# Another order of the last passes of three feed-forward norms: four low parts ahead of a reciprocal, two high parts ahead of a square root

## The chip, the cores and the metric

The kernel runs on one core of a Trainium2 chip. The metric is device time in microseconds (us), the median of several executions. The engines are TensorE (PE in the profile; its weight loads are PEld), VectorE (DVE), ScalarE (ACT), GpSimd (POOL) and SyncE (SP), which issues the loads of the weights.

## The reference

A sequence of 512 tokens with 1024 features goes through a first block of two layers and then a second block of one layer. Only the first block's feed-forward parts and the norms behind them matter here; all is float32.

```python
def layer_norm(x, g, b):
    mu = jnp.mean(xf, axis=-1, keepdims=True)
    var = jnp.mean(jnp.square(xf - mu), axis=-1, keepdims=True)
    return ((xf - mu) * lax.rsqrt(var + LN_EPS)).astype(x.dtype) * g + b
...
for l in range(DEPTH):        # DEPTH = 2
    x = layer_norm(DEEPNORM_ALPHA * x + 0.5 * swiglu_ffn(x, ffn1...), ln1_g[l], ln1_b[l])
    x = layer_norm(DEEPNORM_ALPHA * x + hybrid_mixer(x, ...), ln2_g[l], ln2_b[l])
    x = layer_norm(DEEPNORM_ALPHA * x + 0.5 * swiglu_ffn(x, ffn2...), ln3_g[l], ln3_b[l])
```

## The kernel before

The activations stay in SBUF with the features on the partitions: `x` is eight tiles (k = 0 to 7, `KT` = 8) of 128 features by the tokens. A float32 product is made of three products of shorter numbers: each weight and each activation is split into a high part (`w_hi`, `x_hi`) and a low part (`w_lo`, `x_lo`), and TensorE adds high by high, low weight by high, and high weight by low.

**The norm.** `LayerNorm` works in two parts of 256 tokens, so that the second part's statistics can be taken while the first part is already being used. The diff, and this text, number the sixteen pieces 0 to 7 (part 0, tile k) and 8 to 15 (part 1). For a part, ScalarE squares the mean (`act_mean2`), VectorE makes the variance (`dve_variance`, L843), ScalarE takes the root (`act_root`, L802) and VectorE the reciprocal (`dve_inverse`, L850). Then each piece passes four steps: `centre` on VectorE (L855, subtracts the mean), `scale` on VectorE (L862, times gain and reciprocal), `act_out` on ScalarE (L809, adds the bias and writes the high part `x_hi`), and `lower` on VectorE (L869, writes the low part `x_lo`). Every engine executes its instructions in the order in which they are written, and waits on semaphores for the others. `centre` waits for the reciprocal of its part, `scale` for its own piece's `centre`, also where both run on VectorE. After the pieces ScalarE adds the bias to `x` itself (`act_moved`, L817).

**Who reads the pieces.** The next stage begins with a group of five output tiles (`pe_group`, L458 and L470). TensorE takes the pieces in the order 0 to 15: for each, the five tiles' high weights by `x_hi` of the piece, then by `x_lo` of it. For the pairs 0, 1 and 8, 9 it does three of the tiles for both pieces first and then the other two. It waits for high(piece) before the first and for low(piece) before the second. Then it multiplies the low weights by `x_hi` (L470), with no further need of the norm.

**Which norms.** `finish_act` and `finish_dve` of `LayerNorm` write the order for the norms of class `FfnNorm`. There are three: behind the first feed-forward of layer 0 (in front of a mixer), behind the second of layer 0 (in front of a feed-forward) and behind the first of layer 1 (in front of a mixer). The mixers' norms and the norm between the two blocks have orders of their own, which the diff does not touch. In the stretch of the diff the other work on VectorE's queue is `dve_split` (L350, low part of a weight tile, which frees the raw tile for SyncE's next load) and `dve_z_last` (L876); on ScalarE's it is `act_split` (L339, high part of a weight tile).

Of the kernel before, what the change touches and what calls it, by code (L numbers as in the profile page):

```python
# [24 lines left out]
KT = D // P  # L25
# [216 lines left out]
def build(nc, t):  # L242

    ctx = ExitStack()
    with ctx:
# [84 lines left out]
        def act_split(until):  # L330

            while turn["act"] <= min(until, len(plan) - 1):
                u = turn["act"]
                turn["act"] += 1
                n, r, s = plan[u][3] * P, u % RAW_SLOTS, slot[u]
                act.wait_ge(*loaded[r].at(u))
                if slot_before[u] is not None:
                    act.wait_ge(*used(slot_before[u]))
                nc.scalar.copy(w_hi[s][:, 0:n], w_raw[r][:, 0:n]).then_inc(*w_high.inc(u))  # L339

        def dve_split(until):

            while turn["dve"] <= min(until, len(plan) - 1):
                u = turn["dve"]
                turn["dve"] += 1
                if u in on_pool:
                    continue
                n, r, s = plan[u][3] * P, u % RAW_SLOTS, slot[u]
                dve.wait_ge(*w_high.at(u))
                nc.vector.tensor_tensor(  # L350
                    w_lo[s][:, 0:n], w_raw[r][:, 0:n], w_hi[s][:, 0:n].bitcast(F32),
                    ALU.subtract).then_inc(*w_low_dve.inc(u))
# [416 lines left out]
        class LayerNorm(Norm):  # L769
# [50 lines left out]
            def finish_act(self):  # L820
                self.act_ready()
                self.act_square_last(0)
                self.act_mean2(0)
                self.act_root(0)
                act_split(self.u_next + 1)
                self.act_out(0, 0)
                self.act_out(1, 0)
                act_split(self.u_next + GROUP)
                self.act_square_last(1)
                act_split(self.u_next + GROUP + 1)  # L830
                self.act_mean2(1)
                self.act_out(2, 0)
                self.act_root(1)
                for k in range(3, KT):
                    self.act_out(k, 0)
                for k in range(KT):
                    self.act_out(k, 1)
                self.act_moved()
# [58 lines left out]
            def finish_dve(self):  # L897
                centre, scale, lower = self.passes()
                self.dve_z_last(0)
                self.dve_variance(0)  # L900
                self.dve_inverse(0)
                centre(0, 1)
                scale(0)
                centre(2)
                scale(1, 2)
                centre(3, 4, 5, 6)
                lower(0, 1)
                self.dve_z_last(1)
                centre(7)
                scale(3, 4, 5)  # L910
                lower(2)
                self.dve_variance(1)
                scale(6, 7)
                self.dve_inverse(1)
                lower(3, 4)
                centre(8, 9)
                lower(5, 6)
                scale(8)
                centre(10, 11)
                scale(9)  # L920
                centre(12)
                scale(10)
                lower(7, 8)
                scale(11, 12)
                lower(9, 10)
                dve_split(self.u_next + 1)
                centre(13, 14)
                lower(11)
                scale(13, 14)
                centre(15)  # L930
                scale(15)
                lower(12, 13, 14, 15)
# [2657 lines left out]
```

## Time and profile before

| what | us |
|---|---|
| median of 3 runs | 3092.43 |
| lowest and highest | 3090.99, 3094.99 |
| the profiled execution's own time | 3093.18 |
| span of its trace, first to last instruction | 3091.9 |
| TensorE busy in the span | 3044.0 |
| VectorE busy | 1422.7 |
| ScalarE busy | 1158.2 |

The profiled execution took 0.75 us more than the median, and 1.28 us of it lie around the span. A busy TensorE is not TensorE at its peak, since matmuls are pipelined; a gap in its weight loads is the plainer sign of a wait. Times on the timelines are us from the start of the span. In a timeline row the first number is the start, the second the time to the end of the last of the instructions that the row joins (x2 is two of them), and the bracket is how long the engine was idle before it, and who ended that. In a row of a stretch the clock is the mean clock that was granted to TensorE, as a share of its full 2.4 GHz.

### The profile page before, as it was taken

What the parts mean: (1) busy time and instruction counts of PE and PEld (TensorE: products, weight loads), DVE (VectorE), ACT (ScalarE), POOL (GpSimd) and SP (SyncE); (2) the same over time, 40 slices, a digit from 0 to 9 for tenths busy, and PEclk for the clock granted to TensorE, in tenths of its full rate; (3) what the DMA queues carried; (4) which work ended last, traced back from release to release, by engine and by line L of the source; (5) the groups of instructions that cost most, each with busy time, mean ns of one, the idle gap of its engine ahead of it and who ended that gap; (6) DMA issues with size and microseconds to landing.
All of it is one profiled execution on the core that took longest, in us unless ns stands there. A gap on an engine that the chain in (4) does not pass through costs nothing.

```text
span 3091.9 us, 39346 instructions
## 1 busy us (share of the span) xinstructions
PE 3044.0 (98%) x16494; PEld 2548.4 (82%) x16494; DVE 1422.7 (46%) x2120; ACT 1158.2 (37%) x1868; POOL 372.3 (12%) x273
## 2 busy tenths in 40 slices
PE   9999999999999999999999999899999999999999
PEld 7888877888888888887788888899999767788888
DVE  4333476653335433356583333744423766554432
ACT  3322366442223322146552221522223456543221
POOL 0000143300001000014320000200002322200000
PEclk9999999999999999999999999999999999999999
DMA  4233221132232322332123233222233211122232
GB/s 161 96 94 89 93 102 58 59 109 96 94 88 71 116 96 92 94 116 69 55 76 105 94 90 97 72 96 89 86 88 103 79 38 35 41 94 93 94 94 77
DMA packets 76496, 269.62 MB, mean 87 GB/s; under 512 B 8720, under 2 KB 9008, under 8 KB 76064
## 3 DMA queue, kind: packets, MB, share of 16 engines
q1 hardware_dynamic: 74448, 260.08, 26.4%
q0 software_dynamic: 1872, 7.04, 0.7%
q8 instruction: 130, 2.13, 0.3%
q14 instruction: 46, 0.38, 0.0%
HBM read 264.97 MB, written 2.11 MB: 86 GB/s over the span
## 4 chain that ended last, share of the span: by engine, by line
PE 90%; DVE 7%; ACT 2%; issue 1%; DMA 0%; SPq 0%; POOL 0%; DVEq 0%; ACTq 0%
PE psum L394 25%; PE psum L397 25%; PE psum L400 25%; PE psum L458 3%; PE psum L470 2%; PE psum L693 1%; PE psum L413 1%; PE psum L417 1%; PE psum L415 1%; PE psum L2837 1%; DVE z_sum L850 1%; DVE x L862 1%; DVE x L855 1%; DVE b_rank L3112 0%; PE psum L1878 0%
## 5 line engine op out<-in xcount | busy, mean ns | idle before, releaser
L350 DVE TENSOR_TENSOR w_lo<-w_raw,w_hi 128x1024 fp32r<-128x1024 f32 (+1 forms) x444 | 555.3, 1252 | 1261.2 <-ACT w_hi L339 1261.1
L394 PE MATMUL psum<-x_hi,w_hi 128*128 128x512 f32 (+1 forms) x2800 | 964.6, 369 | 2.2 <-ACT neg_mean L2908 1.8
L397 PE MATMUL psum<-x_hi,w_lo 128*128 128x512 f32 (+1 forms) x2800 | 949.7, 363 | 0.8 <-DVE w_lo L350 0.8
L400 PE MATMUL psum<-x_lo,w_hi 128*128 128x512 f32 (+1 forms) x2800 | 945.2, 362 | 0.0
L339 ACT CAST w_hi<-w_raw 128x1024 fp32r<-128x1024 f32 (+1 forms) x490 | 503.9, 1029 | 1173.0 <-PE psum L400 1137.0
L394 PEld LDWEIGHTS psum<-x_hi,w_hi 128*128 128x128 f32 x2800 | 500.1, 188 | 109.8 <-issue 18.5
L397 PEld LDWEIGHTS psum<-x_hi,w_lo 128*128 128x128 f32 x2800 | 499.6, 188 | 88.0 <-issue 4.8
L400 PEld LDWEIGHTS psum<-x_lo,w_hi 128*128 128x128 f32 x2800 | 500.3, 189 | 84.6 <-DVE x_lo L3346 0.3
L394 PE MATMUL psum<-h_hi_ffn,w_hi 128*128 128x512 f32 (+1 forms) x792 | 296.9, 375 | 0.0
L397 PE MATMUL psum<-h_hi_ffn,w_lo 128*128 128x512 f32 (+1 forms) x792 | 292.2, 369 | 0.0
L400 PE MATMUL psum<-h_lo_ffn,w_hi 128*128 128x512 f32 (+1 forms) x792 | 290.7, 367 | 0.0
L394 PEld LDWEIGHTS psum<-h_hi_ffn,w_hi 128*128 128x128 f32 x792 | 148.9, 188 | 28.6 <-issue 1.0
L400 PEld LDWEIGHTS psum<-h_lo_ffn,w_hi 128*128 128x128 f32 x792 | 148.7, 188 | 28.2
L397 PEld LDWEIGHTS psum<-h_hi_ffn,w_lo 128*128 128x128 f32 x792 | 148.6, 188 | 27.2 <-issue 1.0
L394 PE MATMUL psum<-h_hi_b_ffn,w_hi 128*128 128x264 f32 (+2 forms) x550 | 148.6, 316 | 0.0
L397 PE MATMUL psum<-h_hi_b_ffn,w_lo 128*128 128x264 f32 (+2 forms) x550 | 148.1, 315 | 0.0
L400 PE MATMUL psum<-h_lo_b_ffn,w_hi 128*128 128x264 f32 (+2 forms) x550 | 147.6, 314 | 0.0
L363 POOL TENSOR_TENSOR w_lo<-w_raw,w_hi 128x1024 fp32r<-128x1024 f32 x46 | 112.1, 2439 | 252.2 <-ACT w_hi L339 252.1
L1028 POOL TENSOR_TENSOR z_sum<-x 128x512 f32<-128x512 f32 x4 | 5.2, 1299 | 1054.7 <-DVE x L1000 1054.7
L575 ACT CAST h_hi_ffn<-hid 128x512 fp32r<-128x512 f32 x88 | 54.6, 621 | 163.8 <-DVE hid L593 163.8
L400 PEld LDWEIGHTS psum<-h_lo_b_ffn,w_hi 128*128 128x128 f32 x550 | 93.2, 188 | 7.1
L394 PEld LDWEIGHTS psum<-h_hi_b_ffn,w_hi 128*128 128x128 f32 x550 | 93.1, 188 | 6.9
(386 smaller groups left out, 3387.5 us busy)
## 6 DMA issues: line engine op xcount, KB each, us to landing
w_raw<-in_ffn_gu SPq DMA_DIRECT2D x176, 512.0 KB, 3.3
w_raw<-in_ffn_down SPq DMA_DIRECT2D x64, 512.0 KB, 3.5
w_raw<-in_w_in SPq DMA_DIRECT2D x44, 512.0 KB, 3.3
w_raw<-in_b_gate SPq DMA_DIRECT2D x44, 512.0 KB, 3.3
w_raw<-in_b_up SPq DMA_DIRECT2D x44, 512.0 KB, 3.3
w_raw<-in_b_down SPq DMA_DIRECT2D x32, 512.0 KB, 3.5
w_raw<-in_ffn_down SPq DMA_DIRECT2D x32, 384.0 KB, 3.1
w_raw<-in_b_in SPq DMA_DIRECT2D x24, 512.0 KB, 3.3
```

Source lines behind the costliest of these rows:

```text
L339: nc.scalar.copy(w_hi[s][:, 0:n], w_raw[r][:, 0:n]).then_inc(*w_high.inc(u))
L350: nc.vector.tensor_tensor(w_lo[s][:, 0:n], w_raw[r][:, 0:n], w_hi[s][:, 0:n].bitcast(F32), ALU.subtract).then_inc(*w_low_dve.inc(u))
L363: nc.gpsimd.tensor_tensor(w_lo[s][:, 0:n], w_raw[r][:, 0:n], w_hi[s][:, 0:n].bitcast(F32), ALU.subtract).then_inc(*w_low_pool.inc(u))
L394: nc.tensor.matmul(out, w_h, hi[:, c], start=first and i == 0, stop=False)
L397: nc.tensor.matmul(out, w_l, hi[:, c], start=False, stop=False)
L400: done = nc.tensor.matmul(out, w_h, lo[:, c], start=False, stop=final and i == n - 1)
L413: nc.tensor.matmul(out, w_h, hi[:, c], start=j == 0, stop=False)
L415: nc.tensor.matmul(out, w_l, hi[:, c], start=False, stop=False)
L417: done = nc.tensor.matmul(out, w_h, lo[:, c], start=False, stop=j == KT // 2 - 1)
L458: nc.tensor.matmul(out, w_h, x_part[:, c], start=first, stop=False, skip_group_check=True)
L470: done = nc.tensor.matmul(out, w_l, x_hi[:, k, c], start=False, stop=k == KT - 1, skip_group_check=True)
L575: nc.scalar.copy(h_hi[:, f - 1, cols], hid[(f - 1) % 2][:, cols]).then_inc(*h_high.inc(f - 1))
```

## The change

In `finish_act` ScalarE makes high parts 3 and 4 ahead of the root of part 1, beside high part 2 which was there before. In `finish_dve` VectorE makes low part 3 and low part 4 ahead of the variance of part 1, and low part 5 between that variance and the reciprocal; the scale of piece 5 moves behind low part 2. Behind the reciprocal the passes of part 1 are interleaved otherwise: the scales of pieces 8 and 9 come directly behind their centring, and low part 6 lies between them. From the split of a weight tile on, the order is as before. No instruction is added or taken out.

```diff
--- before.py
+++ after.py
@@ -830,8 +830,10 @@
                 act_split(self.u_next + GROUP + 1)
                 self.act_mean2(1)
                 self.act_out(2, 0)
+                self.act_out(3, 0)
+                self.act_out(4, 0)
                 self.act_root(1)
-                for k in range(3, KT):
+                for k in range(5, KT):
                     self.act_out(k, 0)
                 for k in range(KT):
                     self.act_out(k, 1)
@@ -907,22 +909,28 @@
                 lower(0, 1)
                 self.dve_z_last(1)
                 centre(7)
-                scale(3, 4, 5)
+                scale(3, 4)
                 lower(2)
+                scale(5)
+                lower(3)
+                scale(6)
+                lower(4)
                 self.dve_variance(1)
-                scale(6, 7)
+                scale(7)
+                lower(5)
                 self.dve_inverse(1)
-                lower(3, 4)
-                centre(8, 9)
-                lower(5, 6)
+                centre(8)
                 scale(8)
+                lower(6)
+                centre(9)
+                scale(9)
+                lower(7, 8)
                 centre(10, 11)
-                scale(9)
+                scale(10)
                 centre(12)
-                scale(10)
-                lower(7, 8)
+                lower(9)
                 scale(11, 12)
-                lower(9, 10)
+                lower(10)
                 dve_split(self.u_next + 1)
                 centre(13, 14)
                 lower(11)
```

## Rows read from the trace of the kernel before

**Rows 1.** Chain that ended last, by engine, from the page.
```profile
PE 90%; DVE 7%; ACT 2%; issue 1%; DMA 0%; SPq 0%; POOL 0%; DVEq 0%; ACTq 0%
```

**Rows 2.** Three stretches: length, busy PE, PEld, DVE, ACT, POOL, clock, DMA share, GB/s.
```profile
380.50:402.30 21.80, 20.74 (x167) 19.97 (x166) 21.18 (x46) 13.33 (x26) 1.67 (x3) 1.00 0.39 138
987.40:1009.20 21.80, 20.75 (x168) 19.97 (x166) 21.19 (x46) 13.33 (x26) 0.00 (x0) 1.00 0.12 38
1361.30:1383.10 21.80, 20.75 (x167) 19.98 (x166) 21.18 (x46) 13.32 (x26) 1.64 (x3) 1.00 0.40 141
```

**Rows 3.** Waits of TensorE over the span: us, times, longest.
```profile
PE psum L458 <- DVE x_lo L869: 5.3, 7, 1.0
```

**Rows 4.** Timeline of TensorE's weight loads, first norm.
```profile
387.45 0.42 PEld L458 LDWEIGHTS psum<-x_lo,w_hi 128*128 128x128 f32 x3 [1.16 <-DVE x_lo L869]
...
388.03 0.42 PEld L458 LDWEIGHTS psum<-x_hi,w_hi 128*128 128x128 f32 x3
...
398.09 0.41 PEld L458 LDWEIGHTS psum<-x_lo,w_hi 128*128 128x128 f32 x3
```

**Rows 5.** Timeline of VectorE, first norm.
```profile
375.22 1.75 DVE L850 RECIPROCAL z_sum<-z_sum 128x256 f32<-128x256 f32 x1 [0.58 <-ACT z_sum L802]
377.01 0.76 DVE L855 SCALAR_TENSOR_TENSOR x<-psum,x 128x256 f32<-128x256 f32 x2
...
381.98 1.26 DVE L862 SCALAR_TENSOR_TENSOR x<-x,gains,z_sum 128x256 f32<-128x256 f32 x3
383.83 0.48 DVE L869 SCALAR_TENSOR_TENSOR x_lo<-x,gains,x_hi 128x256 fp32r<-128x256 f32 x1 [0.58 <-ACT x_hi L809]
384.23 0.42 DVE L843 SCALAR_TENSOR_TENSOR z_sum<-psum,neg_mean 128x256 f32<-128x256 f32 x1
384.56 0.87 DVE L862 SCALAR_TENSOR_TENSOR x<-x,gains,z_sum 128x256 f32<-128x256 f32 x2
385.35 1.74 DVE L850 RECIPROCAL z_sum<-z_sum 128x256 f32<-128x256 f32 x1
387.01 0.78 DVE L869 SCALAR_TENSOR_TENSOR x_lo<-x,gains,x_hi 128x256 fp32r<-128x256 f32 x2
387.71 0.75 DVE L855 SCALAR_TENSOR_TENSOR x<-psum,x 128x256 f32<-128x256 f32 x2
...
393.73 1.21 DVE L350 TENSOR_TENSOR w_lo<-w_raw,w_hi 128x1024 fp32r<-128x1024 f32 x1
...
396.71 0.41 DVE L855 SCALAR_TENSOR_TENSOR x<-psum,x 128x256 f32<-128x256 f32 x1
397.16 0.48 DVE L862 SCALAR_TENSOR_TENSOR x<-x,gains,z_sum 128x256 f32<-128x256 f32 x1
397.56 1.66 DVE L869 SCALAR_TENSOR_TENSOR x_lo<-x,gains,x_hi 128x256 fp32r<-128x256 f32 x4
```

**Rows 6.** Timeline of ScalarE, first norm.
```profile
383.29 0.50 ACT L809 ACTIVATE x_hi<-x,gains 128x256 fp32r<-128x256 f32 x1
384.68 0.51 ACT L802 ACTIVATE z_sum<-z_sum,eps 128x256 f32<-128x256 f32 x1 [0.89 <-DVE z_sum L843]
385.10 2.09 ACT L809 ACTIVATE x_hi<-x,gains 128x256 fp32r<-128x256 f32 x5
...
398.10 5.01 ACT L817 ACTIVATE x<-x,gains 128x512 f32<-128x512 f32 x8
403.01 1.04 ACT L339 CAST w_hi<-w_raw 128x1024 fp32r<-128x1024 f32 x1
```

**Rows 7.** Timeline of TensorE, low weight halves of the first group.
```profile
402.32 5.72 PE L470 MATMUL psum<-x_hi,w_lo 128*128 128x512 f32 x24
407.88 3.88 PE L470 MATMUL psum<-x_hi,own_lo 128*128 128x512 f32 x16
```

**Rows 8.** The same columns, two stretches of the norm between the two blocks.
```profile
1978.00:1982.00 4.00, 1.79 (x8) 1.79 (x9) 4.00 (x10) 3.26 (x9) 1.85 (x3) 0.74 0.00 0
1982.00:1986.00 4.00, 4.00 (x30) 4.00 (x29) 4.00 (x10) 3.27 (x9) 1.45 (x3) 0.84 0.00 0
```

## The prediction

> **What bounds the kernel now.** I read the chain that ended last first: nine tenths of it are TensorE's own work [rows 1], so another engine's order counts only where TensorE stands still for it. The list of TensorE's waits has one line that belongs to this code, L458 waiting for a low part from L869 [rows 3]; its seven waits include those of other norms that share the line. So I went to the three places. The stretch of 21.8 us from TensorE's first use of a norm to its last is the same in all three to 0.01 us per engine [rows 2]; one place can stand for three, and I read the first. The reader should see two things there. First, VectorE is busy 21.2 of 21.8 us, more than TensorE's 20.7: inside this stretch VectorE is a co-bottleneck, though over the whole span it is busy under half. Second, TensorE has one visible wait, 1.16 us in its weight loads, for low part 3, which comes at 387.45 [rows 4]. VectorE had put the 1.66 us between the reciprocal's start and the next start ahead of it [rows 5].
>
> The less visible thing is at the end. Low part 12 is the first of the last four: it starts at 397.56 and lasts 0.47, so it is there at 398.04, and TensorE's loads that need it begin at 398.09 [rows 4, 5]. There is next to no slack. From 388.03 TensorE runs nearly without a gap and meets VectorE again at piece 12. Whoever wants the stretch to end earlier must get low part 12 earlier, not low part 3.
>
> **The change, step by step.** Ahead of low part 12 VectorE does exactly the same instructions before and after; only idle time and the spacing of starts can change. The split at 393.73 and all behind it keep their order, and low part 12 starts 3.83 us after that split (397.56 less 393.73). So I compute when that split starts after the change. Spacings from start to start, from [rows 5]: scale 0.395 (three end after 1.26, one lasts 0.47), lower 0.40, variance 0.33, centre 0.335 (two end after 0.75).
>
> *New idle at low part 2.* It waits for ScalarE's high part 2, which starts at 383.29 and ends at 383.79, whatever VectorE does, because ScalarE has the mean's square of part 1 in front of it [rows 6]. Before, three scales from 381.98 ran under that wait, the next start could have been 383.17, and low part 2 came at 383.83. Now only two run there, and the third comes behind it. Cost 0.40 us.
>
> *Low parts 3 and 4.* ScalarE gives high 3 at 383.69 to 384.20 and high 4 at 384.08 to 384.59, at its spacing of 0.395 (five end after 2.09, one lasts 0.50) [rows 6]. VectorE: low 2 383.83, scale 5 384.23, low 3 384.62, scale 6 385.02, low 4 385.41, variance 385.81, scale 7 386.14. Both high parts are there 0.4 us and more ahead; these waits cost nothing. Low 3 is ready at 385.10 and not just ahead of 387.45: TensorE's wait of 1.16 us goes. High part 3 also comes 1.4 us earlier; I estimate 0.15 us more from that.
>
> *New idle at low part 5.* This is the wait that the change adds. High part 5 stands behind the root of part 1 on ScalarE, and the root waits for the variance, which now ends at 386.23. The root starts at 386.27, high 5 follows 0.42 later as in [rows 6] (384.68 to 385.10) and ends at 387.20, low 5 starts at 387.24. VectorE was free for it at 386.54. Cost 0.70 us. Queued behind it on VectorE are the reciprocal and every pass of part 1.
>
> *The reciprocal.* It starts at 387.64 and not 385.35, 2.3 us later. Directly behind it now stands centre 8, which waits for its result. Before, two low parts stood there: reciprocal to first centre took 2.36 us (385.35 to 387.71) with both low parts in it. Where part 0 does it directly, it is 1.79 (375.22 to 377.01). With two ordinary low parts elsewhere at 0.395 each that makes 2.58. Cost 0.22 us.
>
> *Two scales right behind their own centre.* At piece 15 the trace has such a pair: 396.71 to 397.16, 0.45 us where a centre otherwise takes 0.335. Pieces 8 and 9 are now such pairs. Cost 2 x 0.12 = 0.24 us.
>
> The Trainium skill speaks against these last two terms: "VectorE: DVE Perf Modes", section "The DRAIN you can't avoid", says in substance that each VectorE operation waits for the pipeline to empty in any case, and that a semaphore between two of them costs nothing more. The rows disagree with it here, 0.45 against 0.335; by the page the sum would be only the two idle times, 1.10 us a norm.
>
> *Sum for one norm:* 0.40 + 0.70 + 0.22 + 0.24 = 1.56 us. Low part 12 starts at 399.12 and is ready at 399.6 or so. Followed through, TensorE is first 1.3 us ahead (low 3 at about 386.1 for 387.45), then waits for low 6 (about 1.2 us), for low 9 (0.6), low 11 (0.35) and low 12 (0.85), and goes through piece 12 at about 399.65 and not 398.09. The last pieces come every 0.395 us from VectorE and are used every 1.17 us (a high and a low part, 0.58 each, as 387.45 to 388.03), so they give no further wait.
>
> *Behind it.* ScalarE's `act_moved` and the next weight tile's high part start 1.6 us later too, at about 399.7 and 404.6 in place of 398.10 and 403.01 [rows 6]. TensorE needs that tile only behind its low-weight pass, which ends at 411.76 before [rows 7] and 413.3 then, so 7 us of cover stay. If it were gone, each us too late would be a us of TensorE. SyncE's loads of weights wait for VectorE's splits and move by the same 1.6 us; their cover is the same. No DMA is moved past another, and GpSimd's queue is untouched. What follows hangs on TensorE and moves as a whole, so I count 1.56 us in full, three times: 4.7 us. Against the profiled execution that is 3093.18 + 4.7 = 3097.9; it stood 0.75 us over the median, so the median becomes 3092.43 + 4.7 = **3097.1 us**, 0.15% slower. Faster or slower by 0.2% (6.2 us) is about what a measurement of this kernel can tell from no change, so the likeliest verdict is "same".
>
> *Bounds.* Below, one norm costs 1.10 us if the waits of VectorE on itself are free. Above, the waits for high 3 and high 4, which I take as free with 0.4 us in hand, could each cost their small hand-over of 0.04 us, and every dependent pair could be as dear as the reciprocal's term: about 1.9 us. That is 3.3 to 5.7 us in all. I take 1.56, because each of its terms has a row of the same shape in the same norm.
>
> **The rivals.**
>
> *Own waits are free*, as the page says: 1.10 x 3 = 3.3 us, 3095.7. Against it stand the two starts 0.45 us apart in [rows 5]. Chance 0.10.
>
> *The wait goes and nothing comes back*: TensorE's 1.16 us and the estimated 0.15 us before it, three times 1.3 = 3.9 us, 3088.5. It would need low part 12 not to decide, that is, VectorE with time in hand; the 0.05 us between 398.04 and 398.09 speaks against it. It is the largest gain that the edit can give, and is not enough for 0.2% either. Chance 0.06.
>
> *No net change*: the later reciprocal is absorbed, because later stages wait for something that does not move, such as a transfer. I see no wait of TensorE on a transfer in the list behind these norms. 3092.4, chance 0.08.
>
> *The clock falls* (this one ends on the slower side). TensorE now stands still four times within some 10 us. In the norm between the two blocks, TensorE was busy 1.79 of 4 us, and the granted clock averaged 0.74 in that stretch and 0.84 in the next, which means parts of each at 1.2 GHz in place of 2.4 [rows 8]; that loses 1.04 + 0.64 = 1.7 us. In our stretches it was 1.00 throughout with 1 us of idle time [rows 2]. If one such fall came in each norm, the cost would be 3 x (1.56 + 1.7) = 9.8 us, 3102.2. It decides for "slower" from 0.5 us a norm on. Against it: the idle pieces are at most 1.2 us with full work between. Chance 0.10.
>
> **How the numbers follow.** The forecast has 0.60, the four rivals 0.34; 0.06 is left for delays of the same kind up to 2.5 us a norm. Slower by over 0.2%: the clock, 0.10, most of the remainder, 0.04, and 0.04 for the forecast's own upper end with the scatter of a median whose three runs span 4 us; 0.18. Faster by over 0.2%: no case reaches it, 0.02 for what I have not seen. Same: 0.80. The range must leave out no more than 0.2: below it, the full gain and part of "no change" (0.09), above it the clock's case (0.10). That is 3092.0 to 3100.5.
>
> **What the profile after would show.** Right: TensorE's wait for low part 3 is gone and waits for low 6, 9, 11 and 12 stand in its place, over 2.5 us of idle loads a norm; VectorE has about 1 us of idle time before low part 2 and 0.7 before low part 5; the reciprocal starts 2.3 us later, the split behind low 10 about 1.6 us later; the stretch of 21.8 us becomes 23.3. The prediction is wrong if low part 12 comes at its old time, if the idle time at low part 5 is missing, if a scale behind its own centre starts after 0.335 us, or if the clock in a stretch is under 1.00.

## The result and the profile after

| | us |
|---|---|
| before, median of 19 runs | 3092.86 |
| after, median of 19 runs | 3097.93 (3095.93 to 3098.99) |
| ratio | 1.0016, 95% interval 1.0010 to 1.0022 |
| span of the profiled execution after | 3097.1 |

The change costs 5.1 us, 0.16%; the interval of the ratio, in us, is 3.1 to 6.8. (One of the 19 runs before, at 7664 us, is not in the ratio.)

**The three stretches.** The next two fences give the weight loads of TensorE at the two ends of a stretch, from its first load of the group to its first low-weight load: the kernel before at the first norm, and then the kernel after with its waits between.

```profile
380.54 0.42 PEld L458 LDWEIGHTS psum<-x_hi,w_hi 128*128 128x128 f32 x3
...
402.21 2.85 PEld L470 LDWEIGHTS psum<-x_hi,w_lo 128*128 128x128 f32 x13
```

```profile
380.36 0.42 PEld L458 LDWEIGHTS psum<-x_hi,w_hi 128*128 128x128 f32 x3
...
385.88 0.43 PEld L458 LDWEIGHTS psum<-x_lo,w_hi 128*128 128x128 f32 x3
...
390.61 0.42 PEld L458 LDWEIGHTS psum<-x_lo,w_hi 128*128 128x128 f32 x3 [1.12 <-DVE x_lo L871]
...
394.04 0.42 PEld L458 LDWEIGHTS psum<-x_lo,w_hi 128*128 128x128 f32 x3 [0.47 <-DVE x_lo L871]
...
397.42 0.42 PEld L458 LDWEIGHTS psum<-x_lo,w_hi 128*128 128x128 f32 x3 [0.27 <-DVE x_lo L871]
...
399.46 0.41 PEld L458 LDWEIGHTS psum<-x_lo,w_hi 128*128 128x128 f32 x3 [0.79 <-DVE x_lo L871]
...
403.61 1.46 PEld L470 LDWEIGHTS psum<-x_hi,w_lo 128*128 128x128 f32 x7
```

Before, 402.21 - 380.54 = 21.67 us; after, 403.61 - 380.36 = 23.25 us, that is 1.58 us more. At the second norm it is 21.71 and 23.25, at the third 21.70 and 23.27: 4.7 us for the three. The wait for low part 3 is gone; that load at 385.88 has no bracket, and from the first load it comes 1.39 us sooner than the one at 387.45 in [rows 4]. Four waits stand in its place, for low parts 6 (1.12), 9 (0.47), 11 (0.27) and 12 (0.79): 2.65 us for 1.16. A bracket counts from the end of the load before; the next load could have started earlier than that end, 0.24 us behind the start of a group of two and 0.35 us behind one of three. So each wait really costs about 0.07 us more than its bracket. The busy times of the three stretches, in the columns of [rows 2]:

```profile
380.36:403.61 23.25, 21.31 (x167) 19.99 (x166) 21.55 (x46) 13.22 (x26) 1.67 (x3) 1.00 0.39 128
987.27:1010.52 23.25, 21.29 (x166) 19.96 (x165) 21.55 (x46) 13.22 (x26) 0.00 (x0) 1.00 0.09 30
1362.73:1386.00 23.27, 21.32 (x166) 20.02 (x165) 21.57 (x46) 13.23 (x26) 1.64 (x3) 1.00 0.39 132
```

The granted clock is 1.00 in all three. In the list of TensorE's waits the line of [rows 3] has become the one below. It counts the idle time of the multiplications, which is shorter than that of the loads, so its rise of 2.5 us is not the cost of the change.

```profile
PE psum L458 <- DVE x_lo L871: 7.8, 13, 1.0
```

**VectorE, first norm after** (lines below the diff are two further down than before, so L871 is the low part, L864 scale, L857 centre, L852 the reciprocal, L845 the variance):

```profile
381.79 0.88 DVE L864 SCALAR_TENSOR_TENSOR x<-x,gains,z_sum 128x256 f32<-128x256 f32 x2
383.65 0.48 DVE L871 SCALAR_TENSOR_TENSOR x_lo<-x,gains,x_hi 128x256 fp32r<-128x256 f32 x1 [0.98 <-ACT x_hi L809]
...
385.97 0.47 DVE L864 SCALAR_TENSOR_TENSOR x<-x,gains,z_sum 128x256 f32<-128x256 f32 x1
387.03 0.49 DVE L871 SCALAR_TENSOR_TENSOR x_lo<-x,gains,x_hi 128x256 fp32r<-128x256 f32 x1 [0.58 <-ACT x_hi L809]
387.43 1.75 DVE L852 RECIPROCAL z_sum<-z_sum 128x256 f32<-128x256 f32 x1
389.21 0.42 DVE L857 SCALAR_TENSOR_TENSOR x<-psum,x 128x256 f32<-128x256 f32 x1
389.67 0.48 DVE L864 SCALAR_TENSOR_TENSOR x<-x,gains,z_sum 128x256 f32<-128x256 f32 x1
...
390.47 0.42 DVE L857 SCALAR_TENSOR_TENSOR x<-psum,x 128x256 f32<-128x256 f32 x1
390.92 0.48 DVE L864 SCALAR_TENSOR_TENSOR x<-x,gains,z_sum 128x256 f32<-128x256 f32 x1
...
395.08 1.23 DVE L350 TENSOR_TENSOR w_lo<-w_raw,w_hi 128x1024 fp32r<-128x1024 f32 x1
...
398.93 1.67 DVE L871 SCALAR_TENSOR_TENSOR x_lo<-x,gains,x_hi 128x256 fp32r<-128x256 f32 x4
```

The reader should see five things, beside [rows 5]; this trace runs 0.18 us ahead at the start of the stretch. The idle time ahead of low part 2 is 0.98 where it was 0.58. The variance has moved behind low part 4, and low part 5 waits for its high part with 0.58 us of idle time. The reciprocal starts at 387.43, so 2.26 us later from the first load than before. The centre directly behind it starts 1.78 us after it; the scales behind their own centre start 0.46 and 0.45 us after it. The split stands at 395.08 (1.53 us later) and low part 12 at 398.93 (1.55 us later). ScalarE shows why low part 5 waits:

```profile
383.12 1.30 ACT L809 ACTIVATE x_hi<-x,gains 128x256 fp32r<-128x256 f32 x3
386.09 0.51 ACT L802 ACTIVATE z_sum<-z_sum,eps 128x256 f32<-128x256 f32 x1 [1.68 <-DVE z_sum L845]
386.50 1.29 ACT L809 ACTIVATE x_hi<-x,gains 128x256 fp32r<-128x256 f32 x3
...
399.47 5.01 ACT L817 ACTIVATE x<-x,gains 128x512 f32<-128x512 f32 x8
404.38 1.03 ACT L339 CAST w_hi<-w_raw 128x1024 fp32r<-128x1024 f32 x1
```

ScalarE stood idle for 1.68 us until the variance let the root start, and high part 5 can only start behind it, at 386.50. The bias adds at 399.47 and the next weight tile's high part at 404.38 are 1.55 us later than in [rows 6], and TensorE does not wait for them.

### The profile page after: what moved, and what is told of

Its sections match the earlier page's. It is cut to its first block, busy times and chain, and to the rows that moved or that the text cites. A ratio compares the mean times of both kernels' runs of the same rounds, so it can differ in the third digit from the quotient of the medians.

```text
span 3097.1 us, 39346 instructions
## 1 busy us (share of the span) xinstructions
PE 3046.3 (98%) x16494; PEld 2549.0 (82%) x16494; DVE 1424.9 (46%) x2120; ACT 1158.2 (37%) x1868; POOL 372.3 (12%) x273
## 4 chain that ended last, share of the span: by engine, by line
PE 88%; DVE 8%; ACT 2%; issue 1%; DMA 0%; SPq 0%; POOL 0%; DVEq 0%; ACTq 0%
PE psum L394 25%; PE psum L397 25%; PE psum L400 25%; PE psum L458 2%; PE psum L470 2%; DVE x L864 1%; PE psum L413 1%; PE psum L417 1%; PE psum L415 1%; DVE x L857 1%; PE psum L693 1%; PE psum L2845 1%; DVE z_sum L852 1%; DVE x_lo L871 1%; DVE b_rank L3120 0%
```

## The experiments

The measure of each is the stretch of TensorE's weight loads in the first norm, as above; it repeats to 0.1 us over the three norms and the whole time scatters by some us. "All" is the ratio to the kernel before, with its interval where there were several rounds.

| kernel | first load | first low-weight load | stretch | all |
|---|---|---|---|---|
| before | 380.54 | 402.21 | 21.67 | |
| after | 380.36 | 403.61 | 23.25 | 1.0016 (1.0010 to 1.0022) |
| e1, scale 5 under the wait | 380.40 | 403.21 | 22.81 | 1.0014 (1.0004 to 1.0023) |
| e2, reciprocal first | 380.52 | 403.16 | 22.64 | 1.0009 (0.9999 to 1.0019) |
| e3, no own pairs | 380.59 | 403.53 | 22.94 | 1.0013 (1.0004 to 1.0022) |
| e7, the three together | 380.54 | 402.48 | 21.94 | one run |
| e4, ScalarE's order alone | 380.44 | 402.08 | 21.64 | 0.9998 (0.9989 to 1.0007) |
| e5, low parts 3 and 4 early, no more | 380.36 | 402.02 | 21.66 | 1.0002 (0.9993 to 1.0012) |
| e8, split under the wait | 380.39 | 402.50 | 22.11 | one run |
| e9, e5 and e8 together | 380.52 | 402.35 | 21.83 | one run |
| e6, order by when TensorE wants it | 380.05 | 400.33 | 20.28 | 0.9986 (0.9977 to 0.9995) |

### What each part of the change costs: e1, e2, e3 and e7

**e1**, the changed kernel with the scale of piece 5 back under the wait for high part 2.

```diff
-                scale(3, 4)
+                scale(3, 4, 5)
                 lower(2)
-                scale(5)
                 lower(3)
```

> The changed kernel with the scale of piece 5 put back ahead of low part 2, where it runs under the wait for high part 2; all else as changed. From TensorE's first weight load of the group to the first low-weight load the kernel before took 21.67 us (380.54 to 402.21), the changed one 23.25 (380.36 to 403.61). Theory (low part 12 decides the end, and every us of VectorE ahead of it counts): 0.40 us less in each norm, 22.85 us, and 3.5 us over the kernel before in all. Rival (only the wait at low part 5 costs): no change, 23.25 us, as that wait stays 0.6 to 0.7 us long.

VectorE's timeline in e1:

```profile
381.84 1.27 DVE L864 SCALAR_TENSOR_TENSOR x<-x,gains,z_sum 128x256 f32<-128x256 f32 x3
383.69 0.88 DVE L871 SCALAR_TENSOR_TENSOR x_lo<-x,gains,x_hi 128x256 fp32r<-128x256 f32 x2 [0.58 <-ACT x_hi L809]
...
386.67 0.48 DVE L871 SCALAR_TENSOR_TENSOR x_lo<-x,gains,x_hi 128x256 fp32r<-128x256 f32 x1 [0.58 <-ACT x_hi L809]
```

Idle time ahead of low part 2 is 0.58 again, that ahead of low part 5 is unchanged at 0.58, and the stretch is 22.81 us, 0.44 less than the changed kernel's. The rival, with the whole cost at low part 5 (no change, 23.25), falls.

**e2**, the changed kernel with the reciprocal ahead of low part 5.

```diff
-                lower(5)
                 self.dve_inverse(1)
+                lower(5)
                 centre(8)
```

> The changed kernel with the reciprocal of part 1 ahead of low part 5. The wait for high part 5 behind the root goes; a shorter one of the reciprocal for the root (about 0.27 us) takes its place, and the reciprocal has a low part behind it again and not a centre. Theory: 0.64 us less in each norm, 22.6 us for the stretch, and 2.8 us over the kernel before in all. Rival (the late reciprocal costs nothing, the cost is in TensorE's gaps): 23.25 us as changed.

VectorE's timeline in e2:

```profile
386.12 0.48 DVE L864 SCALAR_TENSOR_TENSOR x<-x,gains,z_sum 128x256 f32<-128x256 f32 x1
386.78 1.75 DVE L852 RECIPROCAL z_sum<-z_sum 128x256 f32<-128x256 f32 x1 [0.18 <-ACT z_sum L802]
388.45 0.39 DVE L871 SCALAR_TENSOR_TENSOR x_lo<-x,gains,x_hi 128x256 fp32r<-128x256 f32 x1
388.75 0.42 DVE L857 SCALAR_TENSOR_TENSOR x<-psum,x 128x256 f32<-128x256 f32 x1
```

The 0.58 us of idle time has become 0.18 us for the root, a low part stands behind the reciprocal, and the centre starts 1.97 us after the reciprocal with that low part in between. The stretch is 22.64 us, 0.61 less, as forecast (0.64). The interval of the ratio reaches just below 1, so the whole time alone would not tell it from the kernel before.

**e3**, the changed kernel with centres 8 and 9 together.

```diff
-                centre(8)
+                centre(8, 9)
                 scale(8)
                 lower(6)
-                centre(9)
                 scale(9)
                 lower(7, 8)
```

> The changed kernel with the centres of pieces 8 and 9 next to each other, so that no scale stands directly behind its own centre. Theory (such a pair costs 0.12 us): 0.24 us less in each norm, 23.0 us for the stretch. Rival (own waits are free, as the page of the Trainium skill has it): 23.25 us, the same start-to-start times.

VectorE's timeline in e3:

```profile
389.43 0.75 DVE L857 SCALAR_TENSOR_TENSOR x<-psum,x 128x256 f32<-128x256 f32 x2
390.10 0.48 DVE L864 SCALAR_TENSOR_TENSOR x<-x,gains,z_sum 128x256 f32<-128x256 f32 x1
...
395.05 1.22 DVE L350 TENSOR_TENSOR w_lo<-w_raw,w_hi 128x1024 fp32r<-128x1024 f32 x1
```

Two centres and the start of the scale take 0.67 us (389.43 to 390.10), where a centre and its own scale alone took 0.46. The split is 0.26 us earlier than in the changed kernel, if the later start of this trace is counted (395.05 - 380.59 for 395.08 - 380.36), and the stretch is 22.94 us, 0.31 less (0.23 and 0.31 less at the other norms). Had own waits been free, the start-to-start times would have stayed the same; they did not.

**e7**, the three edits at once, against the changed kernel.

```diff
-                scale(3, 4)
+                scale(3, 4, 5)
                 lower(2)
-                scale(5)
                 lower(3)
...
-                lower(5)
                 self.dve_inverse(1)
-                centre(8)
+                lower(5)
+                centre(8, 9)
                 scale(8)
                 lower(6)
-                centre(9)
                 scale(9)
```

> The changed kernel with the three edits of e1, e2 and e3 at once. Their measured savings in the first norm are 0.44, 0.61 and 0.31 us, 1.36 in all. Theory (the terms add up, as all lie on one chain): 21.9 us from TensorE's first weight load of the group to the first low-weight load, 1.36 below the changed kernel's 23.25. Rival (they overlap, or another engine sets a floor between them): clearly above that, 22.5 us or more.

The stretch is 21.94 us, 1.31 below the changed kernel; the three savings sum to 1.36. The terms add, as they do on one chain, and the rival (22.5 us or more) falls. What is left to the kernel before, 0.27 us, has the size of what still stands, the reciprocal's wait for the root:

```profile
385.77 0.47 DVE L864 SCALAR_TENSOR_TENSOR x<-x,gains,z_sum 128x256 f32<-128x256 f32 x1
386.43 1.75 DVE L852 RECIPROCAL z_sum<-z_sum 128x256 f32<-128x256 f32 x1 [0.19 <-ACT z_sum L802]
```

After the scale at 385.77 the next could start at 386.16 and starts at 386.43, so 0.27 us. (The bracket, 0.19, counts from the end of the scale and not from the next possible start.)

### What is not the cause: e4

**e4**, the kernel before with ScalarE's half alone.

```diff
                 self.act_out(2, 0)
+                self.act_out(3, 0)
+                self.act_out(4, 0)
                 self.act_root(1)
-                for k in range(3, KT):
+                for k in range(5, KT):
```

> The kernel before with ScalarE's half of the change alone: high parts 3 and 4 ahead of the root of part 1, VectorE's order untouched. The root waits for the variance until 384.68 in any case, and both high parts end ahead of that. Theory (the cost is in VectorE's order): no change, 21.67 us for the stretch. Rival (the later root is the loss): the reciprocal would start later than 4.8 us behind the first load of the group (385.35 less 380.54) and the stretch would grow by as much.

The stretch is 21.64 us and the ratio 0.9998: ScalarE's order alone costs and gives nothing. The reciprocal starts 4.81 us behind the first load, as before (385.25 less 380.44). The wait for low part 3 is 1.32 us and no longer 1.16, since high part 3 comes earlier and low part 3 does not; the prediction had estimated 0.15 us for that.

### Where the gain went: e5, e8, e9 and e6

**e5**, e4 with low parts 3 and 4 ahead of the variance.

```diff
                 scale(3, 4, 5)
-                lower(2)
+                lower(2, 3, 4)
                 self.dve_variance(1)
                 scale(6, 7)
                 self.dve_inverse(1)
-                lower(3, 4)
-                centre(8, 9)
                 lower(5, 6)
+                centre(8, 9)
                 scale(8)
```

> The kernel before with high parts 3 and 4 ahead of the root and low parts 3 and 4 ahead of the variance, and nothing else of the change: the reciprocal is not held up by a root behind a low part, and all behind it keeps its order. TensorE's wait of 1.16 us for low part 3 should go. Theory (low part 12 decides): low part 12 comes at its old time, so later waits take all of it back: 21.67 us for the stretch and no change against the kernel before, 0 +- 0.3 us in all. Rival (the wait for low part 3 is itself the loss): 20.4 us, and 3.9 us faster in all.

In the kernel before, low part 7 was made and taken like this (rows of VectorE and of the weight loads):

```profile
391.35 0.87 DVE L869 SCALAR_TENSOR_TENSOR x_lo<-x,gains,x_hi 128x256 fp32r<-128x256 f32 x2
...
392.17 0.43 PEld L458 LDWEIGHTS psum<-x_lo,w_hi 128*128 128x128 f32 x3
```

In e5, all waits of TensorE's weight loads (L458) in the first norm's stretch:

```profile
391.70 0.42 PEld L458 LDWEIGHTS psum<-x_lo,w_hi 128*128 128x128 f32 x3 [1.04 <-DVE x_lo L871]
...
397.92 0.41 PEld L458 LDWEIGHTS psum<-x_lo,w_hi 128*128 128x128 f32 x3 [0.28 <-DVE x_lo L871]
```

This is the change's gain without its costs. The wait for low part 3 is gone, and all of it comes back, 1.04 us at low part 7 and 0.28 at low part 12, together the 1.32 us of e4; the stretch is 21.66 us and the ratio 1.0002. So the wait that the profile shows was not worth its length: taking it away alone gives nothing. The expectation named low part 12; the larger part came back earlier, at 7.

**e8**, the kernel before with the split of a weight tile under the wait for high part 2.

```diff
                 scale(3, 4, 5)
+                dve_split(self.u_next + 1)
                 lower(2)
...
                 lower(9, 10)
-                dve_split(self.u_next + 1)
                 centre(13, 14)
```

> The kernel before with one thing moved: the split of a weight tile (1.14 us) from behind low part 10 into the idle time ahead of low part 2. Low part 12 comes 0.66 us earlier, and all from low part 2 to low part 10 comes 0.48 us later, low part 3 too. Theory (in the kernel before the wait for low part 3 and low part 12 both bind, 0.05 us apart): TensorE waits 0.48 us longer for low part 3 and has nothing to win it back with, 22.15 us for the stretch. Rival (low part 12 alone decides): 21.0 us.

All waits of TensorE's weight loads (L458) in the first norm's stretch:

```profile
385.96 0.41 PEld L458 LDWEIGHTS psum<-x_hi,w_hi 128*128 128x128 f32 x3 [0.56 <-ACT x_hi L809]
...
387.77 0.41 PEld L458 LDWEIGHTS psum<-x_lo,w_hi 128*128 128x128 f32 x3 [1.15 <-DVE x_lo L869]
```

VectorE has no idle time here and low part 12 starts 0.66 us earlier (396.75 with this trace's start at 380.39), yet the stretch is 0.44 us longer: low part 3 comes that much later. The wait is in two brackets now, 0.56 for high part 3 and 1.15 for low part 3. So low part 12 alone does not decide (21.0 us): in the kernel before, low part 3 binds too.

**e9**, e5 with the same split, against e5.

```diff
                 scale(3, 4, 5)
+                dve_split(self.u_next + 1)
                 lower(2, 3, 4)
...
-                dve_split(self.u_next + 1)
                 centre(13, 14)
```

> The kernel of e5 (low parts 3 and 4 ahead of the variance, else as before) with the split moved as in e8. Low parts 3 and 12 now both come early, but low part 7 stays behind three scales and five centres and comes 0.48 us later. Theory (each low part has its own due time): TensorE waits at low part 7 about 1.5 us and gains nothing, 21.8 us for the stretch, so the gain of e6 needs its order of the middle pieces too. Rival (the two ends decide, the middle does not): 20.4 us as in e6.

All waits of TensorE's weight loads (L458) in the first norm's stretch:

```profile
388.68 0.42 PEld L458 LDWEIGHTS psum<-x_lo,w_hi 128*128 128x128 f32 x3 [0.23 <-DVE x_lo L871]
...
392.32 0.41 PEld L458 LDWEIGHTS psum<-x_lo,w_hi 128*128 128x128 f32 x3 [1.23 <-DVE x_lo L871]
```

Low parts 3 and 12 both come early and still nothing is gained, 21.83 us: 0.23 us of waiting at low part 5 and 1.23 at low part 7. So the middle has its own due times: low part 7 starts 0.44 us later from the first load than in e5 (391.77 less 380.52, for 391.17 less 380.36).

**e6**, ScalarE as changed and VectorE in the order of TensorE's wants, from low part 2 on.

```diff
-                lower(2)
-                self.dve_variance(1)
-                scale(6, 7)
-                self.dve_inverse(1)
-                lower(3, 4)
-                centre(8, 9)
-                lower(5, 6)
-                scale(8)
-                centre(10, 11)
-                scale(9)
-                centre(12)
-                scale(10)
-                lower(7, 8)
-                scale(11, 12)
-                lower(9, 10)
                 dve_split(self.u_next + 1)
-                centre(13, 14)
-                lower(11)
-                scale(13, 14)
-                centre(15)
-                scale(15)
-                lower(12, 13, 14, 15)
+                lower(2)
+                self.dve_variance(1)
+                lower(3, 4)
+                scale(6, 7)
+                lower(5)
+                self.dve_inverse(1)
+                lower(6)
+                centre(8, 9)
+                scale(8)
+                lower(7)
+                scale(9)
+                lower(8)
+                centre(10, 11)
+                lower(9)
+                scale(10)
+                centre(12)
+                scale(11)
+                lower(10)
+                scale(12)
+                lower(11)
+                centre(13, 14)
+                lower(12)
+                scale(13, 14)
+                centre(15)
+                lower(13)
+                scale(15)
+                lower(14, 15)
```

> ScalarE as changed; VectorE in the order in which TensorE wants the pieces: the split of a weight tile fills the idle time ahead of low part 2, the variance stands behind low part 2, low parts 3 and 4 behind it, low part 5 ahead of the reciprocal, and low parts 12 and 13 are no longer behind the scales of 14 and 15. Theory (a low part is late only because of what stands ahead of it on VectorE): each low part comes ahead of its use, TensorE has no wait behind piece 2, 20.4 us for the stretch, 1.3 us a norm and 3.9 us in all faster than the kernel before. Rival (TensorE's start-up of the group has a floor of its own, or the later work takes the gain back): 21.7 us for the stretch, or 20.4 us with no gain in the whole.

VectorE's timeline at the place that was idle, and then TensorE's weight loads: both ends of the stretch and its only waits.

```profile
381.49 1.26 DVE L864 SCALAR_TENSOR_TENSOR x<-x,gains,z_sum 128x256 f32<-128x256 f32 x3
382.68 1.21 DVE L350 TENSOR_TENSOR w_lo<-w_raw,w_hi 128x1024 fp32r<-128x1024 f32 x1
383.81 0.47 DVE L871 SCALAR_TENSOR_TENSOR x_lo<-x,gains,x_hi 128x256 fp32r<-128x256 f32 x1
```

```profile
380.05 0.42 PEld L458 LDWEIGHTS psum<-x_hi,w_hi 128*128 128x128 f32 x3
...
381.29 0.30 PEld L693 LDWEIGHTS psum<-x,ones 128*128 128x128 f32 x2 [0.31 <-DVE x L878]
381.74 0.30 PEld L693 LDWEIGHTS psum<-square,ones 128*128 128x128 f32 x2 [0.15 <-ACT square L724]
...
400.33 1.69 PEld L470 LDWEIGHTS psum<-x_hi,w_lo 128*128 128x128 f32 x8
```

The split fills the idle time, low part 5 stands ahead of the reciprocal without waiting (the root was started early, behind a variance directly behind low part 2), and TensorE has no wait behind the two sums of the norm itself (L693). The stretch is 20.28 us, 20.25 at both other norms: 1.4 us less a norm, 4.3 us in all. The median is 3089.53 against 3093.35 beside it, 3.8 us faster; the interval of the ratio lies wholly below 1. This kernel is the fastest of all, 0.14% under the kernel before.

## Why the prediction was right

Forecast 3097.1 us, measured 3097.93; forecast 4.7 us over before, measured 5.1 with an interval of 3.1 to 6.8. The whole time confirms the size only roughly; the three stretches confirm it closely, with 1.58, 1.54 and 1.57 us for the 1.56 forecast.

| step | forecast, us a norm | in the trace after | by experiment |
|---|---|---|---|
| idle time ahead of low part 2 | 0.40 | 0.40 (0.98 less 0.58) | 0.44 (e1) |
| waiting at low part 5 | 0.70 | 0.67 (386.36 to 387.03) | with the next row, less the root's 0.27, 0.61; forecast 0.64 (e2) |
| centre directly behind the reciprocal | 0.22 | 0.21 (1.78 to the centre and 0.79 for two low parts, less 2.36 before) | 0.20 (e2: 1.97 for 1.78 and 0.395) |
| two own pairs | 0.24 | 0.24 (0.46 and 0.45 for 0.335) | 0.31 (e3) |
| low part 12 later | 1.56 | 1.55 | 1.31 undone and 0.27 left (e7) |

(386.36 is the start of the scale at 385.97 and its spacing of 0.395.) e2 undoes the wait and gives the reciprocal a low part as its neighbour again, but puts a wait of 0.27 us for the root in their place, which is why it gives less than the two rows' sum.

**That low part 12 decides** is shown for the changed kernel: it comes 1.55 us later and the stretch is 1.58 longer. For the kernel before it is half the story, and the prediction's advice to get "low part 12 earlier, not low part 3" is wrong as it stands. With low part 3 early the gain came back mostly at low part 7 (e5), and with low part 12 early and low part 3 late the stretch was longer (e8). In the kernel before, TensorE waits for low part 3, takes low part 7 at 392.17, 0.35 us after it is ready (it starts at 391.35 and lasts 0.47), low part 9 at 393.82, 0.41 us after it is ready (made from 392.94), and low part 12 0.05 us after. The prediction had the first and the last of these; those in the middle were missed. That did not move its number, because low part 12, behind them, has less in hand than either.

**TensorE's later waits** came at low parts 6, 9, 11 and 12 as forecast; the brackets sum to 2.65 us, where I had about 3.0. That is a difference in counting: from the time at which each load could have started, the delays are 1.19, 0.54, 0.34 and 0.85 us, against 1.2, 0.6, 0.35 and 0.85 forecast.

**One reading was too wide.** The three stretches are not the same "to 0.01 us per engine": that holds for TensorE, VectorE and ScalarE, but GpSimd works 1.67, 0.00 and 1.64 us in them, and the transfers' share is 0.39, 0.12 and 0.40 [rows 2]. The cost was the same in all three, so neither bore on it.

**Behind the stretches** the forecast that all moves as a whole is shown in one place. What TensorE does from the end of the second stretch to the start of the third takes 352.21 us before (1009.09 to 1361.30) and 352.21 after (1010.52 to 1362.73).

**The rivals.** *Own waits are free*: 1.10 us a norm; the pairs at 0.45 and e3 speak against it: 0.335 us to the next start became 0.45 when that one waited for the result. The Trainium skill's "VectorE: DVE Perf Modes", section "The DRAIN you can't avoid", reports from eight tensor copies that "the semaphore costs nothing extra here"; this case's trace does not agree with that for its instructions. The same section also says that a next operation which is not held starts earlier, a sentence that the prediction left out, and the 0.335 us agree with it: that start lies ahead of the end of the centre before it, which lasts 0.41 us. *The wait goes and nothing comes back*: e5 shows that it comes back even where the change's own cost is left out. *No net change*: the interval excludes it. *The clock falls*: it was 1.00 in all three stretches, with up to 1.13 us of waiting at a time.

**The span of the profiled execution** rose by 5.2 us, of which the stretches explain 4.7. The rest did not move as a whole. Between the first two norms the changed kernel won 1.5 us back (from 402.21 to 987.38 before is 585.17 us, from 403.61 to 987.27 after 583.66), and behind the third it lost 2.2. That these nearly cancel is luck. Most of both is TensorE's clock in the mixers. Their windows, before and then after, in the columns of [rows 2]:

```profile
440.00:450.00 10.00, 8.00 (x40) 5.62 (x39) 5.96 (x8) 3.88 (x13) 2.51 (x2) 0.87 0.15 52
1422.00:1434.00 12.00, 10.01 (x71) 7.28 (x68) 6.97 (x13) 6.46 (x20) 3.40 (x2) 1.00 0.16 47
```

```profile
440.00:450.00 10.00, 7.98 (x45) 5.79 (x44) 6.16 (x8) 5.11 (x15) 3.92 (x3) 1.00 0.25 83
1422.00:1434.00 12.00, 9.98 (x48) 7.13 (x47) 7.38 (x10) 5.51 (x16) 4.32 (x3) 0.86 0.23 82
```

In the first mixer part of the stretch was granted at 1.2 GHz before and none of it after; in the second it is the other way round. TensorE's own work does not tell them apart: in each of these windows, in both kernels, it stands still once for 2.0 us, for a result of ScalarE (the multiplications behind it start at 446.50 and 1427.27 before, at 447.91 and 1430.31 after). The same stop of 2.0 to 2.1 us stands at these two places in all eleven traces of this document. In the 6 us behind it the mean clock was 0.72 in 13 of the 22 cases and 1.00 in the other nine, with nothing between. It fell in the first mixer before and in e1, e3, e4, e6, e7 and e9, and from the first norm's stretch to the second's those seven took 585.1 to 585.2 us; the four where it stayed took 583.6 to 583.7. In the second mixer the fall costs 1.56 of the 2.2 us: from the multiplications behind the stop to the next of L1878 (L1886 after) is 4.06 us before (1427.27 to 1431.33) and 5.62 after (1430.31 to 1435.93).

Whether the shift of the norms decides where the clock falls, or chance does, was not tested. Each fall is worth 1.5 us, a third of the whole effect, which is why the stretch, and not the whole time, is the measure of these edits.

## What to carry to other kernels

When two engines are both nearly full in a stretch, a wait that the profile names is worth only what the pieces behind it have in hand, that is, by how much each is ready before it is wanted. Write down when each piece is wanted and when it is made, and look for the second and third that have no slack before taking the first away (here 3, 7, 9 and 12, with 0, 0.35, 0.41 and 0.05 us in hand). A piece that is moved ahead must not bring another engine's round trip in front of a long instruction: low part 5 ahead of the reciprocal waited for a high part behind a root behind a variance. Idle time can be filled for nothing by work that has no due time, such as a weight split, but only if the pieces behind it can bear to come later.

## What was not expected of the hardware

On VectorE an instruction that waits for its predecessor's result starts 0.45 us behind it, where the next independent one starts after 0.335 (128x256, centre). The prediction had read that in one row, and e3 shows it by experiment. The same 0.12 us stands behind the reciprocal: a centre that waits for it starts 1.78 us behind its start, a low part that does not 1.66 to 1.67.

What was not expected is that a low part directly behind a reciprocal lasts 0.38 to 0.39 us where it otherwise lasts 0.47 to 0.48, and that its successor starts 0.30 us behind it and not 0.395: in e2, 388.45 to 388.75. It was in the trace of before too, where the two low parts at 387.01 end after 0.78 us and not 0.87 [rows 5]. It is nearly half of what the reciprocal's neighbour is worth (0.095 of 0.21 us); the rest is the 0.12 us of the centre's wait.
